# Rows of modulation panels moved, a first weight split moved to GpSimd, and a gate moved behind a rotation, in a two-block transformer kernel

## The chip, the cores and the metric

The kernel runs on one core of a Trainium2 chip. The metric is device time in microseconds (us) for one execution, lower is better. A core has TensorE (PE, matmuls; its weight loads are shown as PEld), VectorE (DVE), ScalarE (ACT), GpSimd (POOL), the SyncE queue (SP), and 16 DMA engines that the queues share.

## What is computed

Two diffusion-transformer blocks run one after the other on 256 latent tokens (with 256 context tokens), width 1024, all in float32. The first block has two layers. Each projects a modulated RMS norm of both streams, does two attentions (a low-rank one, MLA, and a neighbourhood one), merges them through gates, and ends with an MLP:

```python
mod_lat = (silu_c @ w_ada[l] + b_ada[l])[:, None, :]
sh1, sc1, gt1, sh2, sc2, gt2 = jnp.split(mod_lat, 6, axis=-1)
h = modulate(rms_norm(x_lat, g_attn[l]), sh1, sc1)
gl, mq, mk, mv, nq, nk, nv = mixer_proj(h, *proj_w)
...
g = jax.nn.sigmoid(gate_logits)
y = g[..., :D_MODEL] * (y_mla @ w_mla_o) + g[..., D_MODEL:] * (y_na @ w_na_o)
x_lat = x_lat + gt1 * (y @ w_out)
x_lat = x_lat + gt2 * squared_relu_mlp(modulate(rms_norm(x_lat, g_mlp[l]), sh2, sc2), w_ff1[l], w_ff2[l])
```

The second block has an mLSTM layer and then a windowed attention layer with 16 query heads and 4 key heads, rotary angles, a sink, and an output gate `silu(z)`, with its own modulation from `ada_w_2`.

## The kernel before

**Number format.** Every weight panel is split on chip into a high part (`whi`, written by ACT in `hi`, line 1106, as float32r) and the rest (`wlo`, a subtraction in `lo_to` on DVE, line 1664, or in `lo` on POOL, line 2285, for the panels named in `POOL_PANELS`). A product takes three matmuls: high by high, high by low, low by high (lines 552 to 554, 573 to 575, 589 to 591, 1024 to 1026). Activations are split the same way.

**Panels.** All weights come as panels of up to 1 MB (`plan`, line 135), in one fixed order, through three raw buffers. SP issues them in order (line 512). It may issue panel i only when panel i-3 has been given back: a weight panel is given back when its second low half is written, a modulation panel ("ada") when TensorE has multiplied with it, since it is used from the raw buffer as it is. `whi` and `wlo` have two buffers each, so the high part of weight n waits until TensorE has finished with weight n-2. In each half panel, TensorE can begin once the first half of the low part is there.

**Modulation.** There are 72 ada panels, numbered by `ADA`; four of them make one row of 1024 modulation values (shift, scale or gate). The first eight (`AT_START`) are at the front; the others are placed behind the weight panels listed in `AFTER`, and TensorE multiplies with each as soon as it is done with that weight (`used`, `ada`, line 606). ACT copies a finished row (`ada_out`, line 1118), TensorE turns it (`rows_out`, line 624) and DVE adds the bias (line 1671).

**The start.** ACT squares the eight chunks of both streams, DVE adds them up (`stat`), TensorE sums over partitions (`rms`, line 635), ACT takes the root, DVE the reciprocal (line 1706). Then `modulate` on DVE (line 1721) goes by chunks k = 0 to 7 of context ("c") and then latents ("l"): `scaled` for k and k+1, `left` for k. ACT writes the high part in `shifted` (line 1156). For odd k, POOL writes the low part in `norm_mod` (line 2295). `scaled` of chunk k waits for the low part of chunk k-4. TensorE takes the first projection panel `cq 0` chunk by chunk in `weight_pair` (lines 573 to 575), the next one, `cq 1`, whole.

**The gates of layer 0.** For each quarter h = 0 to 3 TensorE goes through the panels `gm`, `gn` (8 chunks, 1 MB each), `mo`, `no` (4 chunks, 512 KB each).

**The attention layer.** TensorE projects keys and queries, then z panel 0 (`gate(0)`, banks `atz` 0 and 1), turns the four key heads (`akT`, line 1049), projects z panels 1 and 2, and turns the queries. PSUM banks are given out in turn among six, and TensorE waits until the last holder of a bank has been read. DVE multiplies z by its sigmoid in `gate` (line 2203), which is what reads the `atz` banks, and rotates the query heads in `rotated` (line 2198).

Of the kernel before, what the change touches and what calls it, by code (L numbers as in the profile page):

```python
# [9 lines left out]
ALU = mybir.AluOpType  # L10
# [71 lines left out]
def zones():  # L82
# [9 lines left out]


AT_START = 8
AFTER = ([(kind, 0, h) for h in range(4) for kind in ("gm", "gn", "mo")]
         + [(f"ff{kind}", 0, 4 * g + a) for kind, g in MLP_ORDER for a in range(4)]
         + [("na", 1, a) for a in range(1, 5)] + [(kind, a) for kind in ("mq", "mk") for a in range(4)]
         + [(kind, a) for a in range(4) for kind in ("mo", "mz")])
# [10 lines left out]
    return k % 2 == 1 and (s, x) != ("s0", "c")  # L109


POOL_PANELS = [("uq", 0, 0), ("ff1", 0, 0), ("ckv", 1, 0), ("uq", 1, 0), ("ff1", 1, 0), ("mq", 0), ("atkv", 0)]


class Panel:
# [160 lines left out]
def program(nc, d, out):  # L276
    with ExitStack() as ctx:
# [14 lines left out]
        done = Done()  # L292
# [226 lines left out]
        def tensor(e):  # L519
# [559 lines left out]

            e.wait_ge(*done("ones"))  # L1080
            e.wait_ge(s_const, 16)
            for i in range(AT_START - 1):
                ada(i)
            for x in "cl":
                rms("n1.0", x)
            ada(AT_START - 1)
            first_layer(0)
            first_layer(1)
            lstm_layer()
# [3 lines left out]
        def scalar(e):  # L1093
# [144 lines left out]
            def first_layer(l):  # L1238
# [3 lines left out]
                tiles = [2, 3] if last else [0, 1, 2, 3]  # L1242
                s = f"n1.{l}"
                if not l:
                    for x in "cl":
                        for k in range(8):
                            shifted(s, k, x, "b", 0, 0)
                            if x == "c" and k == 1:
                                hi_to(at["cq", 0, 0].i)
                turned(s, "cl")  # L1250
                for x, kind in enumerate(("ckv", "cq") if last else ("cq", "ckv")):
                    h, gain, c0, acc, n_p = (cqh, S(f"gqa{l}"), q0, 2, 3) if kind == "cq" else (ckh, S(f"gkva{l}"), 0, 3, 1)
# [371 lines left out]
            e.wait_ge(s_x["lat"], 16)  # L1624
            for k in range(8):
                stat("n1.0", k, "cl")
                if k == 4:
                    ada_out(3)
            for x in "cl":
                rms("n1.0", x)  # L1630
            ada_out(AT_START - 1)
            first_layer(0)
            first_layer(1)
            lstm_layer()
# [3 lines left out]
        def vector(e):  # L1638
            nxt, rows, taken = [0], [0], [AT_START]

            def own():

                e.wait_ge(ve.sem, ve.n)
# [190 lines left out]
            def first_layer(l):  # L1834
# [5 lines left out]
                if not l:  # L1840
                    rows_out()
                    fold("b", 0, 1, "gattn0")
                    own()
                    modulate(s, "c", "b", 0, 1, 0, [(lambda: None, lambda: lo_to(at["cq", 0, 0].i))])
                    modulate(s, "l", "b", 0, 1, 0)
                ts(gcol[:, 0], S(f"gmqc{l}"), 96 ** -0.5, None, ALU.mult, None)
                e.tensor_copy(gcol[:, 1], S(f"gmkc{l}")).then_inc(*up(ve, ("gcol", l)))
                e.wait_ge(s_const, 16)
# [341 lines left out]
            def attention_layer():  # L2190
                s = "s1"
                tmp = work[:, :, :].rearrange("p a t -> p (a t)")
                ts(nsink[:, :], S("sink"), -1.0, None, ALU.mult, None)
                cs = C("rope2").rearrange("p (t s f) -> p t s f", t=2, s=2)
                for i, n in enumerate(("atq", "atk")):
                    rope_tables(atabs[:, i], cs, S(n)[:, 0:32], S(n)[:, 32:64])

                def rotated(v, n_h, i, tile, *names):
                    tm = [tmp[:, 512 * k:512 * k + n_h * 32].rearrange("p (h f) -> p h f", f=32) for k in range(4)]
                    tab = [atabs[:, i, k, tile].unsqueeze(1).to_broadcast([128, n_h, 32]) for k in range(4)]  # L2200
                    rope(v[:, :, 0:32], v[:, :, 32:64], tab, tm, *names)

                def gate(a):
                    for c in range(2 * a, 2 * a + 2):
                        e.wait_ge(*done(("asig", c)))
                        tt(sz[:, c, :], banks(("atz", c))[:, 0:256], sz[:, c, :], ALU.mult, ("read", ("atz", c)))

                begin(at["atkv", 0])
                begin(at["atkv", 1])
                for tile in range(4):  # L2210
                    e.wait_ge(*done(("aksq", tile)))
                    e.tensor_reduce(ass_[:, 0, tile], work[:, tile, 0:256].rearrange("p (h e) -> p h e", e=64), AX.X,
                                    ALU.add).then_inc(*up(ve))
                rsqrt_fine(ass_[:, 1], ass_[:, 0], ass_[:, 2], 64, "aks", "akrt")
                for tile in range(4):
                    tt(qk[:, tile], qk[:, tile], ass_[:, 1, tile].unsqueeze(2).to_broadcast([128, 4, 64]), ALU.mult)
                begin(at["atq", 0])
                own()
                for tile in range(4):
                    v = qk[:, tile]  # L2220
                    if tile < 2:
                        tt(v, v, S("atk").unsqueeze(1).to_broadcast([128, 4, 64]), ALU.mult)
                    else:
                        rotated(v, 4, 1, tile - 2)
                    own()
                    e.tensor_copy(kd[:, tile, :, 0, :], v).then_inc(*up(ve))
                    e.tensor_copy(kd[:, tile, :, 1, :], v).then_inc(*up(ve, ("k heads", tile)))
                begin(at["atq", 1])
                for half in range(2):
                    r = slice(half * 8, half * 8 + 8)  # L2230
                    for tile in range(2):
                        e.wait_ge(*done(("aqsq", half, tile)))
                        e.tensor_reduce(asums[:, tile, r], aPT[half][:, tile, :].rearrange("p (h e) -> p h e", e=64), AX.X,
                                        ALU.add).then_inc(*up(ve))
                    rsqrt_fine(arms[:, :, r], asums[:, :, r], ascr[:, :, r], 64, ("aqs", half), ("aqrt", half))
                    begin(at["atz", 0] if half else at["atq", 2])
                    if half:
                        gate(0)
                    for tile in range(2):
                        rotated(aqtok[:, tile, half * 512:half * 512 + 512].rearrange("p (h e) -> p h e", e=64), 8, 0, tile,  # L2240
                                ("q heads", half))
                        if tile == 0 and half == 0:
                            begin(at["atq", 3])
                for a in range(1, 3):
                    begin(at["atz", a])
                    gate(a)
                own()

                def among_units(i):
                    if i == 1:  # L2250
                        gate(3)
                    if i in (16, 17):
                        lo_to(at["atw", i - 16].i)

                softmax("A", at_units(), ast, among_units)
                gate_lo(7)
                for a in range(4):
                    begin(at["atw", a])
                    for j in range(2):
                        residual("at", 2 * a + j, ("atw", 2 * a + j), "s", 1, 2, "l")  # L2260
# [20 lines left out]
        def gpsimd(e):  # L2281
            def lo(p):
                for a in range(2):
                    e.wait_ge(*done(("hi", p.i, a)))
                    e.tensor_tensor(p.half(wlo[p.buf], a), p.half(raw[p.slot], a), p.half(whi[p.buf], a).bitcast(F32),  # L2285
                                    ALU.subtract).then_inc(*up(po, ("lo", p.i, a)))

            def rsqrt(o, i, ready, *names):

                e.wait_ge(*done(ready))  # L2290
                e.tensor_scalar(o, i, EPS, None, ALU.add).then_inc(*up(po))
                e.wait_ge(po.sem, po.n)
                e.tensor_tensor(o, o, power[:, :], ALU.pow).then_inc(*up(po, *names))

            def norm_mod(s, parts):
                for x in parts:
                    a, b, _ = PARTS[x]
                    for k in range(1, 8, 2):
                        e.wait_ge(*done(("xhi", s, k, x)))
                        e.tensor_tensor(XAl[:, k, a:b], work[:, k % 4, a:b], XAh[:, k, a:b].bitcast(F32), ALU.subtract).then_inc(  # L2300
                            *up(po, ("xlo", s, k, x)))

            for l in range(2):
                q0 = CTX if l else 0
                if l:
                    lo(at["ckv", l, 0])
                norm_mod(f"n1.{l}", "cl")
                lo(at["uq", l, 0])
                lo(at["ff1", l, 0])
                norm_mod(f"n2.{l}", "l" if l else "cl")  # L2310
            lo(at["mq", 0])
            e.wait_ge(*done(("ff2 end", 1, 3)))
            e.wait_ge(*done(("sum", "s0", "l")))
            e.dma_start(zone[:, :], d["zones"]).then_inc(s_zone, 16)
            norm_mod("s0", "l")
            for i in range(16):
                ssc = col[:, i % 4, 14:15]
                rsqrt(ssc, ssc, ("h mean", i), ("h root", i))
            lo(at["atkv", 0])
            norm_mod("s1", "cl")  # L2320
# [71 lines left out]
```

## Time and profile before

| | |
|---|---|
| median of 3 runs | 2172.58 us (2172.06 to 2174.23) |
| the profiled execution, its own time | 2172.58 us |
| its span in the profile | 2170.8 us |
| PE busy | 2077.5 us, 96% |
| DVE busy | 1132.4 us, 52% |
| ACT busy | 906.0 us, 42% |
| POOL busy | 79.3 us, 4% |
| mean granted TensorE clock | 0.984 |
| read from HBM | 273.01 MB, 127 GB/s |

The span is the time between the first and the last instruction; the device time has 1.8 us more around it. Busy times of different engines overlap. A bracket behind a row of a timeline is the idle time of that engine before it, and what ended it. A granted clock of 1.00 is 2.4 GHz, 0.50 is 1.2 GHz.

### The profile page before, as it was taken

Reading aid. Unit: us, or ns where it says so; the run is one execution under the profiler, and the core shown is the slowest. Engines: PE = TensorE matmul, PEld = TensorE weight load, DVE = VectorE, ACT = ScalarE, POOL = GpSimd, SP = SyncE. Lnnn points to the kernel's source line nnn. Section 1 sums busy time; section 2 is a strip of 40 time slices with the busy share of each in tenths; the row PEclk is TensorE's granted clock in tenths of the full one; section 3 lists DMA queues with packets and bytes.
Section 4 is the critical chain, followed back from the end, with each engine's and each line's share of the span. In section 5 each row is a group of like instructions: output and inputs, shape, how many; then the busy total and the mean of one; then the engine's idle time right before and its main releaser. Section 6 shows DMA issues by size and latency. Waiting matters only on the chain.

```text
span 2170.8 us, 32405 instructions
## 1 busy us (share of the span) xinstructions
PE 2077.5 (96%) x13362; PEld 1727.6 (80%) x13362; DVE 1132.4 (52%) x2150; ACT 906.0 (42%) x1639; POOL 79.3 (4%) x91
## 2 busy tenths in 40 slices
PE   5998999999999999999999899999999799999998
PEld 3897767778777777798779899987877577888977
DVE  4447562336433343465555677642466444445876
ACT  4445662324322231255564555433333222233575
POOL 1000000002000000110000100010000000001000
PEclk8999999999999999999999999999999999999999
DMA  7222004642444444344105445444211044222311
GB/s 282 102 88 75 34 18 148 220 158 78 165 184 155 187 163 168 143 165 180 54 35 197 173 182 186 176 157 160 117 59 57 2 174 175 90 105 78 117 59 40
DMA packets 47106, 277.19 MB, mean 128 GB/s; under 512 B 4464, under 2 KB 12784, under 8 KB 16752
## 3 DMA queue, kind: packets, MB, share of 16 engines
q1 hardware_dynamic: 42080, 266.94, 32.6%
q10 hardware_dynamic: 4736, 7.34, 1.0%
q8 instruction: 106, 1.74, 0.3%
q0 software_dynamic: 144, 0.85, 0.1%
q14 instruction: 40, 0.33, 0.0%
HBM read 273.01 MB, written 2.10 MB: 127 GB/s over the span
## 4 chain that ended last, share of the span: by engine, by line
PE 85%; DVE 7%; ACT 4%; DMA 1%; issue 1%; POOL 0%; SPq 0%; ACTq 0%; DVEq 0%
PE ps L552 18%; PE ps L553 18%; PE ps L554 18%; PE ps L589 4%; PE ps L590 4%; PE ps L591 4%; PE ps L669 3%; PE ps L619 3%; PE ps L705 2%; PE ps L692 2%; DVE t L1646 2%; PE ps L983 2%; DVE t L1664 2%; DMA t<-in_panels 1%; DVE t L1655 1%
## 5 line engine op out<-in xcount | busy, mean ns | idle before, releaser
L552 PE MATMUL ps<-t 128*128 128x512 f32 (+1 forms) x2232 | 779.7, 349 | 6.4 <-DVE t L1664 4.2
L553 PE MATMUL ps<-t 128*128 128x512 f32 (+1 forms) x2232 | 770.4, 345 | 0.0
L554 PE MATMUL ps<-t 128*128 128x512 f32 (+1 forms) x2232 | 769.9, 345 | 0.0
L1664 DVE TENSOR_TENSOR t<-t 128x1024 fp32r<-128x1024 f32 (+2 forms) x364 | 407.4, 1162 | 440.6 <-ACT t L1106 439.9
L1106 ACT ACTIVATE t<-t 128x1024 fp32r<-128x1024 f32 (+2 forms) x378 | 359.6, 1000 | 368.9 <-DMA t<-in_panels 293.1
L552 PEld LDWEIGHTS ps<-t 128*128 128x128 f32 x2232 | 422.3, 189 | 84.0 <-issue 17.1
L554 PEld LDWEIGHTS ps<-t 128*128 128x128 f32 x2232 | 422.3, 189 | 52.9
L553 PEld LDWEIGHTS ps<-t 128*128 128x128 f32 x2232 | 422.5, 189 | 50.1
L1646 DVE TENSOR_TENSOR t<-t 128x512 f32<-128x512 f32 (+9 forms) x637 | 249.3, 411 | 196.2 <-ACT t L1195 51.8
L589 PE MATMUL ps<-t 128*128 128x256 f32 (+1 forms) x812 | 241.2, 297 | 0.3 <-DVE t L1664 0.3
L590 PE MATMUL ps<-t 128*128 128x256 f32 (+1 forms) x812 | 234.8, 289 | 0.0
L591 PE MATMUL ps<-t 128*128 128x256 f32 (+1 forms) x812 | 234.7, 289 | 0.0
L1195 ACT ACTIVATE t<-ps 128x256 f32<-128x256 f32 (+1 forms) x254 | 113.2, 458 | 284.5 <-PE ps L554 154.7
L589 PEld LDWEIGHTS ps<-t 128*128 128x128 f32 x812 | 157.1, 193 | 8.1 <-issue 3.3
L590 PEld LDWEIGHTS ps<-t 128*128 128x128 f32 x812 | 157.0, 193 | 3.2 <-issue 1.7
L591 PEld LDWEIGHTS ps<-t 128*128 128x128 f32 x812 | 157.0, 193 | 1.4
L1655 DVE SCALAR_TENSOR_TENSOR t<-ps,t 128x256 f32<-128x256 f32 (+2 forms) x176 | 83.1, 496 | 112.1 <-PE ps L554 92.7
L1646 DVE TENSOR_TENSOR t<-ps,t 128x512 f32<-128x512 f32 (+5 forms) x150 | 63.1, 427 | 113.0 <-ACT t L1229 56.5
L619 PE MATMUL ps<-t 128*32 128x256 f32 x1152 | 82.1, 405 | 16.9 <-DMA t<-in_panels 16.2
L1218 ACT ACTIVATE t<-ps,t 128x512 f32<-128x512 f32 (+1 forms) x128 | 86.8, 688 | 13.4 <-DVE t L1646 11.5
L1655 DVE SCALAR_TENSOR_TENSOR t<-t 128x256 f32<-128x256 f32 (+5 forms) x194 | 82.5, 456 | 12.6 <-ACT t L1164 10.4
L2285 POOL TENSOR_TENSOR t<-t 128x1024 fp32r<-128x1024 f32 (+1 forms) x14 | 31.8, 2295 | 1556.7 <-ACT t L1106 1556.7
(149 smaller groups left out, 1793.4 us busy)
## 6 DMA issues: line engine op xcount, KB each, us to landing
t<-in_panels SPq DMA_DIRECT2D x236, 1024.0 KB, 4.8
t<-in_panels SPq DMA_DIRECT2D x19, 512.0 KB, 4.3
t<-in_panels SPq DMA_DIRECT2D x6, 768.0 KB, 4.3
t<-in_window ACTq DMA_DIRECT2D x4, 768.0 KB, 4.2
t<-in_ctxT SPq DMA_DIRECT2D x1, 1024.0 KB, 12.4
t<-in_xT SPq DMA_DIRECT2D x1, 1024.0 KB, 14.7
t<-in_ctxT ACTq DMA_DIRECT2D x1, 1024.0 KB, 5.6
t<-in_xT ACTq DMA_DIRECT2D x1, 1024.0 KB, 7.3
```

The source lines that it names most:

```text
L552: e.matmul(o, hi[:, k, w], xh[:, c0:c1], start=k == 0, stop=False)
L553: e.matmul(o, hi[:, k, w], xl[:, c0:c1], start=False, stop=False)
L554: t = e.matmul(o, lo[:, k, w], xh[:, c0:c1], start=False, stop=k == p.nk - 1)
L589: e.matmul(o, xh[:, r], hi[:, k, n0:n1], start=k == 0, stop=False)
L590: e.matmul(o, xh[:, r], lo[:, k, n0:n1], start=False, stop=False)
L591: t = e.matmul(o, xl[:, r], hi[:, k, n0:n1], start=False, stop=k == p.nk - 1)
L619: t = e.matmul(o[32 * j:32 * j + 32, 0:256], sc[kind][:, 2 * q + k, :], w[:, k, j * 256:j * 256 + 256], start=q == 0 and k == 0, stop=q == ...
L1106: e.activation(p.half(whi[p.buf], a), p.half(raw[p.slot], a), ACT.Copy).then_inc(*up(se, ("hi", p.i, a)))
L1195: e.activation(o, i, func, scale=scale).then_inc(*up(se, ("read", key), *names))
L1646: e.tensor_tensor(o, a, b, op).then_inc(*up(ve, *names))
L1655: e.scalar_tensor_tensor(o, a, s_, b, o1, o2).then_inc(*up(ve, *names))
L1664: e.tensor_tensor(p.half(wlo[p.buf], a), p.half(raw[p.slot], a), p.half(whi[p.buf], a).bitcast(F32), ALU.subtract).then_inc(*up(ve, ("lo", ...
```

## The change

Five edits, in four places of the program.

1. `AFTER`: in layer 0 the twelve ada panels 8 to 19 stood behind `gm`, `gn`, `mo` of h = 0 to 3; now they stand behind `gm`, `gn`, `mo`, `no` of h = 0 to 2. The order of the load, of TensorE's work, of `ada_out` and of `rows_out` follows.
2. The low part of the first weight panel, `cq 0` of layer 0, is made on POOL in place of DVE, ahead of POOL's first `norm_mod`.
3. At the start TensorE multiplies with ada panels 0 to 3, does both `rms` sums, and then ada panels 4 to 7; before, ada 0 to 6, the sums, ada 7. ACT copies row 0 behind the last square, ahead of the roots, in place of amid the squares.
4. ACT writes the high part of `cq 0` ahead of all `shifted` chunks, in place of behind chunk 1.
5. In the attention layer DVE's `gate(0)` moves from ahead of the rotation of the second half of the query heads to behind it.

```diff
-AFTER = ([(kind, 0, h) for h in range(4) for kind in ("gm", "gn", "mo")]
+AFTER = ([(kind, 0, h) for h in range(3) for kind in ("gm", "gn", "mo", "no")]
...
-POOL_PANELS = [("uq", 0, 0), ...
+POOL_PANELS = [("cq", 0, 0), ("uq", 0, 0), ...
@@ tensor
-            for i in range(AT_START - 1):
+            for i in range(4):
                 ada(i)
             for x in "cl":
                 rms("n1.0", x)
-            ada(AT_START - 1)
+            for i in range(4, AT_START):
+                ada(i)
@@ scalar, first_layer
                 if not l:
+                    hi_to(at["cq", 0, 0].i)
                     for x in "cl":
                         for k in range(8):
                             shifted(s, k, x, "b", 0, 0)
-                            if x == "c" and k == 1:
-                                hi_to(at["cq", 0, 0].i)
@@ scalar, start
             for k in range(8):
                 stat("n1.0", k, "cl")
-                if k == 4:
-                    ada_out(3)
+            for i in range(4):
+                ada_out(i)
             for x in "cl":
                 rms("n1.0", x)
-            ada_out(AT_START - 1)
+            for i in range(4, AT_START):
+                ada_out(i)
@@ vector, first_layer
+                    lo_to(at["cq", 0, 0].i)
                     own()
-                    modulate(s, "c", "b", 0, 1, 0, [(lambda: None, lambda: lo_to(at["cq", 0, 0].i))])
-                    modulate(s, "l", "b", 0, 1, 0)
+                    for x in "cl":
+                        modulate(s, x, "b", 0, 1, 0)
@@ vector, attention_layer
                     begin(at["atz", 0] if half else at["atq", 2])
-                    if half:
-                        gate(0)
                     for tile in range(2):
                         rotated(aqtok[...], 8, 0, tile, ("q heads", half))
...
-                for a in range(1, 3):
-                    begin(at["atz", a])
+                for a in range(3):
+                    if a:
+                        begin(at["atz", a])
                     gate(a)
@@ gpsimd
-                if l:
-                    lo(at["ckv", l, 0])
+                lo(at["ckv" if l else "cq", l, 0])
                 norm_mod(f"n1.{l}", "cl")
```

## Rows read from the trace of the kernel before

**Rows 1.** The page: busy time of TensorE; and its chain, by engine.
```profile
PE 2077.5 (96%) x13362; PEld 1727.6 (80%) x13362; DVE 1132.4 (52%) x2150; ACT 906.0 (42%) x1639; POOL 79.3 (4%) x91
...
PE 85%; DVE 7%; ACT 4%; DMA 1%; issue 1%; POOL 0%; SPq 0%; ACTq 0%; DVEq 0%
```

**Rows 2.** Timeline, all engines, 2061.5 to 2064.6: start, duration, engine, line, tiles, count.
```profile
2061.83 1.91 PE L1049 MATMUL ps<-t 128*128 128x128 f32 x16
...
2063.28 0.75 DVE L1646 TENSOR_TENSOR t<-ps,t 128x256 f32<-128x256 f32 x2
...
2063.81 0.19 PEld L552 LDWEIGHTS ps<-t 128*128 128x128 f32 x1 [0.30 <-DVE t L1646]
```

**Rows 3.** Timeline of DVE from 2060 to 2105.
```profile
2061.00 2.36 DVE L1664 TENSOR_TENSOR t<-t 128x1024 fp32r<-128x1024 f32 x2
...
2064.06 4.49 DVE L1646 TENSOR_TENSOR t<-t 128x256 f32<-128x256 f32 x12
```

**Rows 4.** Timeline of TensorE: first matmul after two idle times.
```profile
55.80 0.50 PE L552 MATMUL ps<-t 128*128 128x512 f32 x1 [1.53 <-DVE t L1664]
...
914.45 1.19 PE L640 MATMUL ps<-t 128*128 128x256 f32 x2 [4.50 <-DVE t L1646]
```

**Rows 5.** Windows: busy time of each engine, granted clock, DMA share, GB/s.
```profile
24.00:26.00 2.00, 2.00 (x17) 0.60 (x17) 1.70 (x3) 1.57 (x3) 0.00 (x0) 0.50 1.02 410
...
914.00:915.00 1.00, 0.55 (x1) 0.50 (x2) 0.30 (x1) 0.00 (x0) 0.02 (x1) 0.50 0.00 0
...
918.00:919.00 1.00, 1.00 (x7) 1.00 (x7) 0.90 (x3) 0.42 (x2) 0.00 (x0) 0.64 0.00 0
```

**Rows 6.** Timelines of TensorE and ScalarE, layer 0, from 381 to 388.
```profile
381.15 0.51 PE L552 MATMUL ps<-t 128*128 128x512 f32 x1
...
385.80 0.55 ACTq L1399 DMA_DIRECT2D t<-in_xT  x1
...
386.94 1.07 PE L619 MATMUL ps<-t 128*32 128x256 f32 x16
...
387.94 0.50 PE L552 MATMUL ps<-t 128*128 128x512 f32 x1
```

**Rows 7.** Timelines in the MLP of layer 0, four engines, from 556 to 566.
```profile
556.54 1.07 PE L619 MATMUL ps<-t 128*32 128x256 f32 x16
...
557.67 0.80 SPq L512 DMA_DIRECT2D t<-in_panels  x2
...
562.34 2.01 ACT L1106 ACTIVATE t<-t 128x1024 fp32r<-128x1024 f32 x2 [3.65 <-DMA t<-in_panels]
...
563.44 2.36 DVE L1664 TENSOR_TENSOR t<-t 128x1024 fp32r<-128x1024 f32 x2 [4.02 <-ACT t L1106]
```

**Rows 8.** Timelines at the start of the kernel, three engines, in order of time.
```profile
23.04 0.38 ACT L1125 ACTIVATE t<-ps 128x256 f32<-128x256 f32 x1 [0.94 <-PE ps L619]
...
24.03 2.34 DVE L1646 TENSOR_TENSOR t<-t 128x512 f32<-128x512 f32 x3 [1.00 <-ACT t L1143]
...
24.10 3.86 PE L619 MATMUL ps<-t 128*32 128x256 f32 x32
...
31.08 3.54 DVE L1706 RECIPROCAL t<-t 128x256 f32<-128x256 f32 x2 [4.71 <-ACT t L1153]
...
31.73 1.07 PE L619 MATMUL ps<-t 128*32 128x256 f32 x16
...
34.95 1.09 DVE L1655 SCALAR_TENSOR_TENSOR t<-t 128x16 f32<-128x16 f32 x3
...
36.95 1.99 ACT L1106 ACTIVATE t<-t 128x1024 fp32r<-128x1024 f32 x2
...
41.35 1.28 DVE L1655 SCALAR_TENSOR_TENSOR t<-t 128x256 fp32r<-128x256 f32 x3 [0.18 <-ACT t L1164]
```

**Rows 9.** Timelines of POOL and DVE ahead of the attention layer.
```profile
1991.71 4.93 POOL L2285 TENSOR_TENSOR t<-t 128x1024 fp32r<-128x1024 f32 x2 [267.19 <-ACT t L1106]
...
1993.16 1.23 DVE L1646 TENSOR_TENSOR t<-t 128x256 f32<-128x256 f32 x1 [0.54 <-ACT t L1143]
```

More of the change, by code:

```diff
@@ L109, in on_pool @@
     return k % 2 == 1 and (s, x) != ("s0", "c")
-POOL_PANELS = [("uq", 0, 0), ("ff1", 0, 0), ("ckv", 1, 0), ("uq", 1, 0), ("ff1", 1, 0), ("mq", 0), ("atkv", 0)]
+POOL_PANELS = [("cq", 0, 0), ("uq", 0, 0), ("ff1", 0, 0), ("ckv", 1, 0), ("uq", 1, 0), ("ff1", 1, 0), ("mq", 0), ("atkv", 0)]
 class Panel:
@@ L2201, in rotated @@
                     rope(v[:, :, 0:32], v[:, :, 32:64], tab, tm, *names)
[L2203 to L2206, printed above, removed]
                 begin(at["atkv", 0])
@@ L2243, in attention_layer, with gate @@
                             begin(at["atq", 3])
-                for a in range(1, 3):
-                    begin(at["atz", a])
+                def gate(a):
+                    for c in range(2 * a, 2 * a + 2):
+                        e.wait_ge(*done(("asig", c)))
+                        tt(sz[:, c, :], banks(("atz", c))[:, 0:256], sz[:, c, :], ALU.mult, ("read", ("atz", c)))
+                for a in range(3):
+                    if a:
+                        begin(at["atz", a])
                     gate(a)
```

## The prediction

> **What bounds the kernel now.** I read the page first, for who is busy. TensorE is, 96% of the span, and the chain that ended last runs 85% through it [rows 1]. So an edit on another engine counts only where it makes TensorE wait, and there it counts in full, for there is next to nothing later in which a wait could be absorbed. I then took the four places of the change one by one, with the timeline of each engine, and asked for each TensorE instruction what it needs and when that is there. The three that matter are the attention layer, the gates of layer 0, and the start. The profiled execution took 2172.58 us, which is also the median, around a span of 2170.8 us, so differences of the span carry over one to one.
>
> **Edit 5, the gate behind the rotation.** The reader should look at TensorE between 2061 and 2064. It turns the four key heads from 2061.83 for 1.91 us, to 2063.74 [rows 2]. Then comes z panel 1. PSUM banks are dealt in turn among six: `atz` 0 and 1, then four `akT`, so `atz` 2 falls on the bank of `atz` 0, and must wait until DVE has read it. DVE reads it in `gate(0)`, two multiplications from 2063.28 to 2064.03, the first done at about 2063.7. TensorE's weight load starts at 2063.81, and it names DVE as what it waited for, 0.30 us [rows 2]. So this wait ends last already, by a hair: there is no slack at all. After the edit DVE ends the split at 2063.36, then does the rotation, twelve operations in 4.49 us [rows 3], and only then `gate(0)`. The first read ends at 2063.3 + 4.5 + 0.4 = 2068.2 in place of 2063.7, and z panel 1 begins 4.5 us late. What gets earlier is the rotated query heads, by 0.75 us. TensorE turns those only behind z panels 1 and 2, some 12 us later, so that is worth nothing. DVE's next split (for z panel 2) comes 0.1 us later, ahead of z panel 1's end by 5 us. Cost: 4.5 us.
>
> The idle time has a second price. Before 914.45 TensorE had idled 4.50 us, about as long [rows 4]; behind it the granted clock was 0.50 and came back within the slice from 918 to 919, whose mean is 0.64, so at 918.7 [rows 5]. For 4.3 us it did half of what it could, which costs 1.7 to 2.1 us. Idle times of a third of that are common in this trace (1.53 us before 55.80 [rows 4]) with the clock at full speed behind them, so I charge this loss to the long stall alone. I take 1.9 us here. If the clock is not lowered, this term is nothing; if it is, 2.1 at most. Edit 5 together: 6.4 us, between 4.4 and 6.6.
>
> **Edit 1, the ada panels of layer 0.** Twelve stay twelve, each still 1.0 us of TensorE (386.94 to 387.94 [rows 6]), so TensorE's work is the same. What moves is who waits for which buffer. Panel i is loaded when panel i-3 is given back. Before, `gm` of quarter h+1 follows `mo`, ada, `no`, and so waits for `mo`'s low part, long done. After, the order is `mo`, ada, `no`, ada, `gm`: it waits for the ada panel behind `mo`, that is until TensorE is done with it. From there to a `gm` that can be multiplied, the MLP has the same pattern: the ada panel ends at 556.54 + 1.07 = 557.61, SP issues at 557.67, the panel has landed when ACT starts on it at 562.34, DVE starts on the low part at 563.44 and has half of its 2.36 us done at 564.62 [rows 7]. That is 7.0 us. In the MLP 11 us of matmuls cover it. Here the cover is `no`: a panel of that size takes 386.94 - 381.15 = 5.8 us, and the ada panel another 1.0 [rows 6], in which the first 0.07 overlap. 6.7 us of cover for 7.0 us: 0.3 to 0.4 us of stall, for h = 0, 1, 2. For h = 1 ACT issues the 1 MB load of `xT` in this stretch, right behind the split of `no` (at 385.80 [rows 6]). It shares the engines with `gm`'s load. At the 410 GB/s of a full stretch [rows 5] one MB takes 2.6 us; a third of that, 0.9 us, is my estimate of the overlap, between nothing and 2.6. Quarter 3 now has no ada panels, but its loads were covered before, so nothing comes back. Rows of modulation are complete earlier, and none was waited for. Sum: 3 x 0.35 + 0.9 = 1.9 us, between 0.5 and 4.
>
> **Edits 2, 3 and 4, the start.** Before, TensorE's two norm sums stood behind ada 6, which waited for its load, and the reciprocals began at 31.08 [rows 8]. DVE's last addition ends at 26.37. With row 0's copy no longer amid the squares (0.94 us idle and 0.38 us of copy on ACT, 1.00 us idle on DVE [rows 8]) it ends at about 25.4. The reciprocals can begin at about 27.0 (I allow 1.6 us for sum and root, an estimate) and end at 30.6 in place of 34.6. That is a gain of 4 us only if the modulation row is there, and here lies the catch. Ada 7 is loaded when ada 4 has been used. Ada 4 started at 24.10, now it stands behind both sums and row 0's turn, at about 28.3. At the granted clock of 0.50 one such panel takes 1.93 us (two took 3.86 [rows 8, 5]), so it is given back at 30.2 in place of 26.0, the load lands 4.7 us later [rows 7], and ada 7 starts at 34.9 in place of 31.73 [rows 8]. Copy, turn and bias take to 37.3, so the first `scaled`, which followed the three operations begun at 34.95 at about 35.2, starts at 37.5.
>
> `cq 0` comes late as well: its slot is that of ada 5, given back at 31.9, and it cannot land before 36.6, more likely at 37.4 since ada 7 lies ahead in the queue. ACT now waits for it ahead of every `shifted`; its split took 1.99 us from 36.95 [rows 8]. Its first half is done at 38.4. DVE is rid of 2.36 us, but POOL takes 4.93 us for the same two halves [rows 9], to 43.4, and its part of `norm_mod` comes behind it: chunk 1's low part at 44.0 or 44.2 (0.6 us by the same rate). `scaled` of chunk 5 waits for it. Before, that was the last of the three operations from 41.35, starting at 42.2 [rows 8]. From there the chunks go at their old pace, so `modulate`, POOL's last chunk, ACT's split of `cq 1` and TensorE's start on it, at 55.80 before [rows 4], all come 1.9 us late. Without POOL's queue it would still be 37.5 against 35.2 less the DVE work saved, about nothing. I take 2.0 us, between -1 and 4.
>
> POOL's work could also slow DVE down. While POOL made such a low part, a DVE addition of two 128x256 tiles took 1.23 us [rows 9], against 4.49 / 12 = 0.37 us in the rotation [rows 3]. Five chunk operations fall under `cq 0`'s split; at 0.86 us more each they would take 4.3 us more, of which 1.9 us are idle on DVE already, waiting for chunk 1: 2.4 us more. This is how the Trainium skill has it (GPSIMD Engine Reference, Key points): the two engines share their interfaces to SBUF, and contend when a DVE instruction has two inputs there. By that rule the start would cost 4.4 us and not 2.0. I keep the 2.0, because these operations also wait for ACT between one another.
>
> **Sum.** 6.4 + 1.9 + 2.0 = 10.3 us: 2172.6 + 10.3 = 2182.9 us.
>
> **Rivals.**
> - *No clock loss, small stalls* (edit 5 at 4.5, edit 1 at 1, start at 0): 2178 us. For it: only one idle time of this length is in my rows. Chance 0.16.
> - *Contention* (start by the DVE operations' stretched time, `gm` behind `xT` in full): 2.4 + 2 more, 2187 us. The 1.23 us speaks for it. Chance 0.13.
> - *The start pays and edit 5 is all that stands against it*: if ada 7 lands by 32, the earlier reciprocals and DVE's 2.36 us give back up to 4 us, and with 4.5 for edit 5 the time is 2173 to 2176, no change. It needs ada 4 to be given back by 27.5, ahead of the sums. Chance 0.05.
> - *The other side, faster*: as the last, and z panel 1 does not wait, because its bank is not the one that `gate(0)` frees. Then 2172.6 - 4 = 2168.6 us. It decides with one fact, the bank, and the 0.30 us wait for DVE speaks against it. Chance 0.02.
> - *The forecast*, 2180 to 2186 us: 0.64.
>
> **How the numbers follow.** The range takes the forecast and most of the two rivals beside it: 2177.5 to 2187.5. A measurement of this kernel can tell about 0.2%, 4.3 us, from no change, so "slower" begins at 2176.9 us. Faster 0.02, same 0.05, slower 0.93.
>
> **What would show it.** Edit 5: TensorE idle for 4.4 us or so at the first matmul of z panel 1, released by DVE's multiplication, followed by some 4 us at a granted clock of 0.50. Edit 1: three waits of TensorE for the low part of `gm`, h = 1 to 3, 0.3 us each, the second the longest, where before there was none. Start: ada 7 near 35, POOL's split of about 5 us from 38.5, the first matmul of `cq 1` near 57.8. I am wrong if z panel 1 starts without a wait, if ada 7 starts before 33, or if `gm`'s loads land in under 4.5 us.

## The result, and the profile of the changed kernel

The changed kernel took 2189.88 us (median of 4, 2188.52 to 2192.39), the kernel before beside it 2172.32 us (4 runs, 2168.26 to 2174.23): ratio 1.0085, 95% interval 1.0068 to 1.0101. That is 17.6 us slower, where 10.3 were predicted, and above the top of the range, 2187.5. The same kernel measured a second time gave the same ratio (below). The profiled execution took 2195.78 us, 5.9 us above the median, around a span of 2193.9 us. So I read a second profile of the kernel too (span 2189.9 us).

The page of the changed kernel, TensorE's row and the chain, against [rows 1]:

```profile
PE 2082.4 (95%) x13362; PEld 1730.7 (79%) x13362; DVE 1133.4 (52%) x2148; ACT 905.7 (41%) x1639; POOL 84.2 (4%) x93
...
PE 83%; DVE 8%; ACT 5%; DMA 2%; issue 1%; POOL 0%; SPq 0%; ACTq 0%; DVEq 0%
```

The span grew by 23.1 us. TensorE is busy for 4.9 us of those with the same instructions (a lower clock); the rest is idle time. Where it lies is seen in TensorE's timeline, at the first matmuls behind idle times (the bracket is the idle time and what ended it), of the changed kernel:

```profile
21.18 1.93 PE L619 MATMUL ps<-t 128*32 128x256 f32 x16 [6.74 <-DMA t<-in_panels]
...
25.67 1.22 PE L640 MATMUL ps<-t 128*128 128x256 f32 x2 [2.56 <-DVE t L1647]
...
36.45 1.07 PE L619 MATMUL ps<-t 128*32 128x256 f32 x16 [3.60 <-DMA t<-in_panels]
...
42.97 0.55 PE L573 MATMUL ps<-t 128*128 128x256 f32 x1 [4.26 <-DVE t L1656]
...
45.95 0.58 PE L573 MATMUL ps<-t 128*128 128x256 f32 x1 [1.37 <-POOL t L2302]
...
60.54 0.50 PE L552 MATMUL ps<-t 128*128 128x512 f32 x1 [1.05 <-DVE t L1665]
...
366.41 0.79 PE L552 MATMUL ps<-t 128*128 128x512 f32 x1 [2.75 <-DVE t L1665]
...
410.75 0.79 PE L552 MATMUL ps<-t 128*128 128x512 f32 x1 [3.43 <-DVE t L1665]
...
452.21 0.50 PE L552 MATMUL ps<-t 128*128 128x512 f32 x1 [0.51 <-DVE t L1665]
...
2085.69 0.36 PE L552 MATMUL ps<-t 128*128 128x256 f32 x1 [4.62 <-DVE t L1647]
```

Lines from 1080 on have moved by one or two: 1647, 1656 and 1665 of DVE were 1646, 1655 and 1664. The first six rows are the start: ada 3, the norm sums, ada 7, chunk 0, chunk 1, `cq 1`. The next three are `gm` of h = 1, 2 and 3, none of which waited before. The last is z panel 1.

The same points in both profiles of the changed kernel, as what each stretch adds to the lag behind the profile of before:

| stretch | predicted | first profile | second profile |
|---|---|---|---|
| start, up to `cq 1` | 2.0 | 4.7 | 6.4 |
| from there to the gates of layer 0 | 0 | 0.9 | 0.0 |
| gates and the MLP's norm, 332 to 517 before | 1.9 | 12.6 | 6.2 |
| from there to z panel 1 | 0 | -1.0 | 0.6 |
| attention: stall, over that of before | 4.5 | 4.5 | 4.5 |
| attention: behind the stall | 1.9 | 1.3 | 1.3 |
| sum (of the spans) | 10.3 | 23.1 | 19.1 |

The rows are rounded, the sums are those of the spans. Edit 5 was right but for 0.6 us of clock. The other two terms were too small, and the one of the gates differs by 6 us from one execution to the next. What makes the stretch between the MLP's norm and z panel 1 differ by 1.6 us is not known.

**The attention layer**, DVE's timeline, TensorE's first weight load of z panel 1, and the windows of the changed kernel (columns as in [rows 5]):

```profile
2080.72 4.49 DVE L1647 TENSOR_TENSOR t<-t 128x256 f32<-128x256 f32 x12
2085.12 0.75 DVE L1647 TENSOR_TENSOR t<-ps,t 128x256 f32<-128x256 f32 x2
...
2085.66 0.19 PEld L552 LDWEIGHTS ps<-t 128*128 128x128 f32 x1 [4.83 <-DVE t L1647]
```

```profile
2083.00:2085.60 2.60, 0.00 (x0) 0.00 (x0) 2.57 (x8) 0.74 (x1) 0.00 (x0) 1.00 0.68 287
...
2085.70:2087.00 1.30, 1.30 (x7) 1.30 (x8) 1.30 (x3) 0.00 (x0) 0.00 (x0) 0.61 0.04 13
2087.00:2088.00 1.00, 1.00 (x7) 1.00 (x6) 1.00 (x2) 0.00 (x0) 0.00 (x0) 0.50 0.00 0
```

The rotation stands ahead of `gate(0)`, its 4.49 us are those of [rows 3], and TensorE starts when the gate's first multiplication is done. The 0.30 us of [rows 2] was the wait of the weight load, so it is to be compared with 4.83 here: 4.5 us more (the 4.62 above is the idle time of the matmuls, which was 0.1 us before). The granted clock was still 1.00 during the wait and fell to 0.50 just behind it.

**The gates.** ScalarE and SP in the changed kernel: SP's issues for `gm` of h = 1 and 2 (with those behind them), ACT's split of `gm` for h = 1, 2, 3, and the load of `xT` (the 7.13 us of an SP row is the time over which its three issues are spread, no landing time):

```profile
356.92 7.13 SPq L512 DMA_DIRECT2D t<-in_panels  x3
...
364.04 2.00 ACT L1107 ACTIVATE t<-t 128x1024 fp32r<-128x1024 f32 x2 [8.59 <-DMA t<-in_panels]
...
398.13 0.55 ACTq L1399 DMA_DIRECT2D t<-in_xT  x1
...
400.59 7.13 SPq L512 DMA_DIRECT2D t<-in_panels  x3
...
408.39 2.00 ACT L1107 ACTIVATE t<-t 128x1024 fp32r<-128x1024 f32 x2 [9.11 <-DMA t<-in_panels]
...
449.84 2.01 ACT L1107 ACTIVATE t<-t 128x1024 fp32r<-128x1024 f32 x2 [6.04 <-DMA t<-in_panels]
```

The chain is the one predicted: ada panel, SP, load, ACT, DVE, TensorE. The load is not: issued at 356.92 it lands at 364.04, 7.1 us, and issued at 400.59, 2.5 us behind `xT`'s, it lands at 408.39, 7.8 us. Only the third took 4.9 us (SP's issue at 444.96), against the 4.7 that I took for all. The packets that began in the first 3.4 us behind `gm`'s issue, by queue (packets, MB, share of the engines' time; q1 is SP's queue, with the panels, q10 is ScalarE's, with `xT`), for h = 2 (400.6 to 404) and then for h = 3 (445 to 448.4):

```profile
q10 hardware_dynamic: 746, 0.75, 74.9%
q1 hardware_dynamic: 10, 0.08, 27.2%
...
q1 hardware_dynamic: 101, 0.81, 67.0%
```

So the two loads did not share: `xT`, issued 2.5 us earlier, had 0.75 MB begin in this time and `gm` 0.08 MB, where `gm` of h = 3 had 0.81 MB. `xT` goes in small packets (1040 for 1.05 MB). Windows of the changed kernel show the second price:

```profile
370.00:372.00 2.00, 2.00 (x6) 1.61 (x5) 1.50 (x3) 0.44 (x1) 0.00 (x0) 0.50 0.71 287
...
373.00:374.00 1.00, 1.00 (x6) 0.84 (x5) 0.55 (x1) 1.00 (x2) 0.00 (x0) 1.00 0.06 25
...
415.00:416.00 1.00, 1.00 (x3) 0.75 (x3) 0.84 (x2) 0.09 (x1) 0.00 (x0) 0.50 0.90 320
```

Behind both long stalls the clock is at its lower level, 0.50, for about 6 us, and `gm` takes 14.2 us, twice, in place of the 11.4 that it takes for h = 1 in the second profile, with the clock full. Stalls of 2.75 + 3.43 + 0.51 us and 2 x 2.8 us make 12.3 of the 12.6.

**The start.** ScalarE's split of `cq 0`, then GpSimd and DVE in the changed kernel; the last row is the view that groups instructions by line and shape from 41.4 to 45.4 (its second operation is cut off by the window), with busy time and mean ns:

```profile
39.05 2.00 ACT L1107 ACTIVATE t<-t 128x1024 fp32r<-128x1024 f32 x2 [1.09 <-DMA t<-in_panels]
...
40.19 4.85 POOL L2287 TENSOR_TENSOR t<-t 128x1024 fp32r<-128x1024 f32 x2 [39.76 <-ACT t L1107]
...
41.49 1.33 DVE L1656 SCALAR_TENSOR_TENSOR t<-t 128x256 fp32r<-128x256 f32 x1 [1.44 <-ACT t L1165]
...
42.74 2.58 DVE L1656 SCALAR_TENSOR_TENSOR t<-t 128x256 f32<-128x256 f32 x1
...
46.90 0.47 DVE L1656 SCALAR_TENSOR_TENSOR t<-t 128x256 f32<-128x256 f32 x1
```

```profile
L1656 DVE SCALAR_TENSOR_TENSOR t<-t 128x256 f32<-128x256 f32 x2 | 3.4, 1758 | 0.0
```

In the kernel before such an operation takes 0.48 us (1.28 for three, [rows 8]). Here one takes 1.33 and the next 2.58 us. GpSimd's two instructions of 2.43 us (the mean) end at 42.5 and 45.0, and DVE's two end at 42.8 and 45.3, each 0.3 us behind one of them. A third takes 0.94 us beside chunk 1's low part. That is not a stretch by a factor: DVE waited until the GpSimd instruction was over, the first time for the rest of one, the second time for nearly a whole one. The Trainium skill states this outright (SBUF — State Buffer, SBUF: two separate sides): of the two engines, the one that starts first has the shared ports for the whole instruction and the other is blocked, for DVE operations with two SBUF inputs. The trace agrees, with these two rows.

The row at 46.90 is `scaled` of chunk 5. It may start when chunk 1's low part is there, which was at 45.90, so it was not this wait that ended last but DVE's own blocked operations, by 1.0 us. In the second profile the first two `scaled` were blocked, 4.99 us for the two, and GpSimd was free again before chunk 1 was ready for it.

### The profile page after: what moved, and what is told of

It reads as the page before. It is cut to its first block, busy times and chain, and to the rows that moved or that the text cites. A ratio compares the mean times of both kernels' runs of the same rounds, so it can differ in the third digit from the quotient of the medians.

```text
span 2193.9 us, 32405 instructions
## 1 busy us (share of the span) xinstructions
PE 2082.4 (95%) x13362; PEld 1730.7 (79%) x13362; DVE 1133.4 (52%) x2148; ACT 905.7 (41%) x1639; POOL 84.2 (4%) x93
## 4 chain that ended last, share of the span: by engine, by line
PE 83%; DVE 8%; ACT 5%; DMA 2%; issue 1%; POOL 0%; SPq 0%; ACTq 0%; DVEq 0%
PE ps L552 18%; PE ps L553 17%; PE ps L554 17%; PE ps L589 4%; PE ps L590 4%; PE ps L591 4%; PE ps L669 3%; PE ps L619 3%; DVE t L1647 2%; PE ps L705 2%; PE ps L692 2%; PE ps L983 2%; DVE t L1665 2%; DVE t L1656 2%; DMA t<-in_panels 2%
## 5 line engine op out<-in xcount | busy, mean ns | idle before, releaser
L2287 POOL TENSOR_TENSOR t<-t 128x1024 fp32r<-128x1024 f32 (+1 forms) x16 | 36.7, 2316 | 1609.3 <-ACT t L1107 1609.3
```

## The experiments

Theories ahead of the runs: *A*, each edit costs what its own buffer or queue makes it wait for, and the costs add up; with it that `xT`'s load delays `gm`, and that ada 7 is late because ada 4 is given back late. *B*, the costs come from something else (the number of ada panels close together, the sums ahead of panels, edits that act only together). The count of executions stands beside each time.

**One edit at a time, on the kernel before (2174.58 us, 26 runs, beside these four).** Edit 5 alone (`gate(0)` behind the rotation):

> Edit 5 alone on the kernel before. Theory: z panel 1 waits 4.5 us for its bank and then about 4 us pass at a granted clock of 0.50, together 6 us, so 2178 us. Rival (the stall is absorbed in the attention that follows, or the clock loss is hidden): 2172 to 2176 us.

2180.44 us (9 runs), ratio 1.0025 [1.0015, 1.0035], 5.9 us more. TensorE's timeline:

```profile
2070.76 0.36 PE L552 MATMUL ps<-t 128*128 128x256 f32 x1 [4.62 <-DVE t L1646]
```

The same stall as in the whole change, and 5.8 us more lag behind the layer than ahead of the stall: 4.5 of stall and 1.3 of clock. The clock fell behind the stall, at about 2071, and was full again at about 2074.6.

Edit 1 alone:

```diff
-AFTER = ([(kind, 0, h) for h in range(4) for kind in ("gm", "gn", "mo")]
+AFTER = ([(kind, 0, h) for h in range(3) for kind in ("gm", "gn", "mo", "no")]
```

> Edit 1 alone. Theory from the trace after: the panel gm of quarters 1, 2 and 3 arrives late by 2.8, 3.4 and 0.5 us, and after each of the two long stalls the granted clock costs another 2.7 us; 12 us in all, 2184 us. Rival A (my prediction): 0.35 us a stall and 0.9 us for the load of xT, 2174 to 2175 us. Rival B: the late landing for quarter 1 (7.1 us from issue) was a chance event of the one profiled execution; then about 6.5 us, 2179 us, and the landing is 4.7 us here.

2180.31 us (6 runs), ratio 1.0030 [1.0017, 1.0042], 5.7 us more, where 1.9 had been predicted, and 12 expected from the stalls of the first profile. Nearest is rival B, 6.5 us: `gm` for h = 1 took 5.7 us to land here, not 7.1, and its stall was 1.28 us, not 2.75. The same with the load of `xT` in the last quarter of layer 0 in place of the second:

```diff
-                    if h == 1:
+                    if h == (1 if last else 3):
                         src = kept
```

> Edit 1 alone, and the load of xT that ACT issues in quarter 1 of layer 0 is issued in quarter 3. Theory that this load makes gm of quarter 2 late: its stall falls from 3.4 us to that of an undisturbed quarter (0.5 us), and its clock loss goes, so 5 to 6 us less than edit 1 alone. Rival (the gm panels are late whatever runs beside them, as in quarter 1): within 1 us of edit 1 alone, the stall stays near 3 us.

2175.72 us (10 runs), ratio 1.0005 [0.9995, 1.0014], 1.1 us more. The timelines of TensorE at `gm` of h = 1, 2, 3, first with `xT` in its place, then with it moved:

```profile
359.35 0.50 PE L552 MATMUL ps<-t 128*128 128x512 f32 x1 [1.28 <-DVE t L1664]
...
401.78 0.79 PE L552 MATMUL ps<-t 128*128 128x512 f32 x1 [4.34 <-DVE t L1664]
...
442.56 0.50 PE L552 MATMUL ps<-t 128*128 128x512 f32 x1 [0.37 <-DVE t L1664]
```

```profile
364.17 0.50 PE L552 MATMUL ps<-t 128*128 128x512 f32 x1 [1.21 <-DVE t L1664]
...
402.66 0.50 PE L552 MATMUL ps<-t 128*128 128x512 f32 x1 [0.41 <-DVE t L1664]
...
441.24 0.50 PE L552 MATMUL ps<-t 128*128 128x512 f32 x1 [0.49 <-DVE t L1664]
```

Of the stalls only the second differs: 4.34 us with `xT`'s load beside `gm`'s, 0.41 without. From the end of the ada panel to ACT's split it was 8.8 us with and 4.8 without. The stall takes the lower clock with it (0.79 us for the first matmul in place of 0.50). So `xT`'s load costs 4.6 of edit 1's 5.7 us by the medians, a little less than expected; between the two profiles the gates differ by 6.2 us. What is left is 1.1 us by the medians, with an interval from -1 to 3. That this is the prediction's 3 x 0.35 is luck: the profile has 1.21 + 0.41 + 0.49 = 2.1 us of stalls, most of it for h = 1.

Edits 2, 3 and 4 together (the start):

> Edits 2, 3 and 4 together, without 1 and 5. Theory from the trace after: the first matmul of cq 1 is 4.7 us later than before, so 2177 us. Rival (my prediction): 2.0 us, 2174 to 2175 us. If the three parts are independent, the sum of the differences of this run and of the two others is that of the whole change, 17 to 18 us.

2178.12 us (10 runs), ratio 1.0017 [1.0008, 1.0027], 3.5 us more. The three parts add up to 15.1 us of 17.6, which the intervals (about 2 us each way on every part) allow.

**The whole change again, its start taken apart, and the whole with `xT` moved (before: 2173.01 us, 19 runs).**

> The changed kernel as it is, a second time, to see which of its stalls repeat. Theory: the late landings of gm in quarters 1 and 2 are in part chance, as the 7.1 us of quarter 1 were 5.7 us with edit 1 alone; here quarter 1 lands 4.8 to 7 us after its issue, quarter 2 nearly 8 or 9 us, quarter 3 near 4.9 us. Time 2188 to 2193 us. Rival: the start makes the queue later, and 7.1 us in quarter 1 comes back to within 0.3 us.

2192.46 us (4 runs), ratio 1.0085 [1.0068, 1.0102]: confirmed. Its profile is the second one of the table. TensorE there, at ada 7, chunk 0, `gm` for h = 1 and 2, and z panel 1:

```profile
38.04 1.94 PE L619 MATMUL ps<-t 128*32 128x256 f32 x16 [5.30 <-DMA t<-in_panels]
...
47.14 0.55 PE L573 MATMUL ps<-t 128*128 128x256 f32 x1 [5.99 <-DVE t L1656]
...
365.16 0.50 PE L552 MATMUL ps<-t 128*128 128x512 f32 x1 [0.77 <-DVE t L1665]
...
406.82 0.80 PE L552 MATMUL ps<-t 128*128 128x512 f32 x1 [3.55 <-DVE t L1665]
...
2081.61 0.36 PE L552 MATMUL ps<-t 128*128 128x256 f32 x1 [4.61 <-DVE t L1647]
```

The stalls beside `xT` (3.55) and in the attention layer (4.61) repeat. The one for h = 1 does not: 0.77 us with the clock full behind it, against 2.75 and 2.8 us of slow matmuls. Its load is the slow one in all five profiles that have edit 1: 5.1 to 7.1 us from SP's issue, against 4.7 to 4.9 us for h = 2 and 3 without `xT` beside them. What makes it slow, and vary, stays open.

> The changed kernel with the load of xT of layer 0 issued in quarter 3 in place of quarter 1. With edit 1 alone this took 4.6 us off. Theory: the same here, 4 to 7 us below the changed kernel, 2184 to 2186 us, the stall of quarter 2 near 0.4 us and its clock loss gone. Rival: with two other edits in the kernel the stall is cause of less, under 2 us.

2185.62 us (4 runs), ratio 1.0061 [1.0044, 1.0078], 6.8 us below the whole change beside it. The stall for h = 2 is 0.41 us there. So `xT`'s load is a piece of the size of edit 5's 5.9 us; which of the two is larger the intervals don't tell.

Edit 3 alone, and edits 2 and 4 alone:

> Edit 3 alone: ada 0 to 3, both sums, ada 4 to 7. Theory: ada 7 starts 4 to 5 us late, since its load waits for ada 4 which now stands behind the sums, and that is most of what the start costs: 2 to 4 us, 2177 to 2178 us. Rival (what costs is the split on GpSimd and its queue): under 1 us here.

> Edits 2 and 4 without 3: the first weight's low part on GpSimd, its high part ahead of the modulated chunks. Theory: the chunks wait for GpSimd's 4.9 us, but DVE is rid of 2.4 us, so it costs 0 to 2 us. Rival (this is what the start costs): 3 us and more.

Edit 3: 2178.17 us (10 runs), ratio 1.0022 [1.0012, 1.0031], 5.2 us more (2 to 4 expected). Edits 2 and 4: 2174.37 us (10 runs), ratio 1.0004 [0.9995, 1.0014]. So it is the order of the panels that costs. (That edit 3 alone shows more than 2, 3 and 4 together, 5.2 against 3.5 us, is within the intervals.) Edits 2 and 4 cost 1.4 us at most likely, and no change can't be excluded. In their profile `cq 1` comes 37.6 us behind ada 3, 2.8 more than before, but ada 7 is 2.2 us later there already, with the panels in their old order: a slow load, not the edits.

**What in edit 3, and what would repair it (before: 2174.15 us, 33 runs).** One ada panel more ahead of the sums:

```diff
-            for i in range(4):
+            for i in range(5):
                 ada(i)
             for x in "cl":
                 rms("n1.0", x)
-            for i in range(4, AT_START):
+            for i in range(5, AT_START):
                 ada(i)
```

> Edit 3 alone, but with ada 0 to 4 ahead of the norm sums and ada 5 to 7 behind them, in place of 0 to 3 and 4 to 7. Theory (the start is late because ada 4 is given back late, and ada 7 is loaded into its buffer): ada 4 is given back some 5 us after ada 3 begins, as before, ada 7 starts within 11.5 us of ada 3 (before 10.7, with edit 3 as made 14.8), the first matmul of cq 1 comes 34.5 to 36 us after ada 3 (before 34.75), and the time is that of the kernel before, 0 to 1.5 us above it. Rival (it is the sums ahead of panels, or row 0's copy behind the squares, that costs): 4 to 5 us above, as with edit 3 alone.

2175.57 us (11 runs), ratio 1.0003 [0.9994, 1.0012], 1.4 us more: the loss is gone, within the interval. TensorE's ada 3, ada 7 and `cq 1`, first with edit 3 as made, then with five panels ahead:

```profile
22.09 1.93 PE L619 MATMUL ps<-t 128*32 128x256 f32 x16 [7.33 <-DMA t<-in_panels]
...
36.84 1.93 PE L619 MATMUL ps<-t 128*32 128x256 f32 x16 [2.56 <-DMA t<-in_panels]
...
61.05 0.50 PE L552 MATMUL ps<-t 128*128 128x512 f32 x1 [1.53 <-DVE t L1666]
```

```profile
22.73 1.94 PE L619 MATMUL ps<-t 128*32 128x256 f32 x16 [7.34 <-DMA t<-in_panels]
...
34.13 1.07 PE L619 MATMUL ps<-t 128*32 128x256 f32 x16 [0.73 <-DMA t<-in_panels]
...
57.24 0.50 PE L552 MATMUL ps<-t 128*128 128x512 f32 x1 [1.54 <-DVE t L1666]
```

Counted from ada 3, ada 7 starts 14.8 us later in the first and 11.4 in the second (10.7 before), and `cq 1` 39.0 and 34.5 (34.75 before). The sums stand ahead of panels and row 0's copy behind the squares in both, so neither is the cause. The buffer of ada 4 is. The earlier sums buy nothing: the modulation row comes no sooner.

Edit 1 with the ada panels behind `gm`, `gn`, `no` of all four quarters, never behind `mo`:

> The twelve ada panels of layer 0 behind gm, gn and no of h = 0 to 3, so never behind mo; on the kernel before. Theory (edit 1 costs because gm's buffer is that of the ada panel behind mo): gm of the next quarter waits only for mo's low part, so no stall of TensorE over 0.3 us at gm, xT's load meets no load that is waited for, no change: within 1 us of the kernel before. Rival (any ada panel close ahead of gm costs, because the loads of gm and the ada panels share the DMA engines): stalls of 1 to 4 us at gm as in edit 1, 2 to 6 us slower.

2174.01 us (11 runs), ratio 1.0000 [0.9991, 1.0009], and no idle time of TensorE over 0.3 us from 334 on in the gates, with `xT` where it was. An ada panel stands right ahead of `gm` here too (though three to a quarter and not four), and `gm` waits for `mo`'s buffer: it is the buffer that counts. `gm`'s load is then issued early, and `xT` finds nothing that is waited for.

Edit 2 alone, ScalarE's order as before:

> Edit 2 alone: the low part of cq 0 on GpSimd ahead of norm_mod, ScalarE's split of cq 0 where it was, behind chunk 1. Theory (GpSimd's 4.9 us ahead of chunk 1's low part hold the chunks up, whatever ScalarE's order): cq 1 comes 2 to 3.5 us later after ada 3 than before, the time is 1 to 3 us above. Rival (it is ScalarE's wait for cq 0 ahead of the shifted chunks that costs in edits 2 and 4): no change, within 0.7 us.

2175.94 us (11 runs), ratio 1.0009 [1.0000, 1.0019], 1.8 us more. GpSimd and DVE there, then TensorE at chunk 1 and `cq 1`:

```profile
39.84 4.84 POOL L2286 TENSOR_TENSOR t<-t 128x1024 fp32r<-128x1024 f32 x2 [39.41 <-ACT t L1106]
...
41.14 3.82 DVE L1655 SCALAR_TENSOR_TENSOR t<-t 128x256 fp32r<-128x256 f32 x2 [1.81 <-ACT t L1164]
```

```profile
45.60 0.58 PE L573 MATMUL ps<-t 128*128 128x256 f32 x1 [1.71 <-POOL t L2301]
...
58.76 0.50 PE L552 MATMUL ps<-t 128*128 128x512 f32 x1 [0.78 <-DVE t L1664]
```

From ada 3 (22.54) `cq 1` comes 36.2 us later, 1.5 more than before, less than the 2 to 3.5 expected. Two DVE operations again take 3.82 us in place of 1.0, and here DVE then waits another 0.62 us for chunk 1's low part. The lean is that it is GpSimd's split and not ScalarE's order, though the interval begins at no change.

All three repairs on the changed kernel (ada behind `gm`, `gn`, `no`; five panels ahead of the sums; `gate(0)` back), with edits 2 and 4 kept:

> The changed kernel with three repairs: ada panels of layer 0 behind gm, gn, no; five ada panels ahead of the sums; gate(0) back ahead of the rotation. Edits 2 and 4 stay. Theory: what is left is the price of edits 2 and 4, 1 to 2 us above the kernel before (2174 to 2175), 14 to 17 us below the changed kernel. Rival (the edits cost something together that no part shows, the sum of the parts having been 15.1 of 17.6 us): 3 to 5 us above the kernel before. If the sums early and the low part on GpSimd help one another, it is below the kernel before.

2175.43 us (11 runs), ratio 1.0005 [0.9996, 1.0014]: 1.3 us above the kernel before, 14 to 17 us below the changed one. The rival, 3 to 5 us left over, is not seen. Whether edits 1, 3 and 5 as made cost something together this run can't tell, since the repairs take all three away; against it speaks that the table of stretches finds nearly all of the loss at the places of the edits. No version tried is faster than the kernel before.

## Why the prediction was wrong, by its own steps

- **Edit 5, right.** 4.5 us of stall predicted, 4.5 found (4.83 for 0.30 at the weight load). The clock: 1.9 predicted, 1.3 found in all three profiles. The edit alone measured 5.9 us for 6.4.
- **Edit 1, the mechanism right, two sizes wrong.** The waits are those for `gm` behind the ada panel, the second the longest. The term that failed is "a third of that, 0.9 us, is my estimate of the overlap", with its bound of 2.6 us: `xT`'s load put 3 to 4 us on `gm`'s, not 0.9 (7.8 us against 4.9 in the first profile, a stall of 4.34 against 0.41 in the edit alone). The estimate had the two loads share the engines; in the trace `gm` had 0.08 MB begin in 3.4 us and `xT` 0.75 MB. The bound of 2.6 us divided bytes by the 410 GB/s of a full stretch [rows 5], while the engines moved 246 GB/s in the mean in those 3.4 us. Second, "landed 4.7 us later" came from a single row [rows 7]; it was right for h = 3, and for h = 1 it was 5.1 to 7.1 us. With 0.3 us of margin missing, each of those goes to the stall in full.
- **The clock, charged in one place and due in three.** "I charge this loss to the long stall alone" failed. My rows had 1.53 us with the clock full and 4.50 with it halved, and nothing between. In the gates, stalls of 2.75, 3.43, 3.55 and 4.34 us all had the low clock behind them, and 1.28 did not. That is 5.6 us of the first profile. An unknown between two rows should have stood in the range, tied to the size of the stalls.
- **The start, the path right, too short.** Ada 7 was to start at 34.9 and started at 36.45: ada 4 stood behind both sums and began at 29.0, not 28.3, and its successor took 5.4 us to come (SP's issue at 31.03), not 4.7; in the second profile it took 7.0 (31.08 to 38.04). `cq 0` behind it landed at 39.05, not at 37.4, and ScalarE had waited 1.09 us for it. So POOL's split, put at 38.5, started at 40.19, and chunk 1's low part, put at 44.0 or 44.2, was there at 45.9: 1.7 us of the 2.7 missed (`cq 1` came at 60.54, not 57.8). The step that failed is, for the most part, again the landing time of 4.7 us. The other 1.0 us is the next item.
- **Contention of GpSimd and DVE, a rival that I sized wrongly.** I took 0.86 us more for each of five operations, and then left it out of the sum. It was three operations of 1.33, 2.58 and 0.94 us, each blocked to the end of a GpSimd instruction, 3.4 us more in all. That "these operations also wait for ACT between one another" did not hide it: `scaled` of chunk 5 began 1.0 us behind the low part that it was said to wait for. So the block cost 1.0 us beyond the queue on GpSimd in the first profile. The rule of the Trainium skill named ahead (GPSIMD Engine Reference, Key points) named the right cause, but that its 4.4 us lie close to the 4.7 found is luck: most of what was missing came from landing times.
- **Nothing found for the other side.** No gain was measured on any edit.

## What to carry to other kernels

Moving a small panel between loads moves the moment at which a buffer comes free, and it is that moment that costs. Before such a move, write down for each late load which item gave its buffer back, and move panels only to where that item is long done; both repairs here (behind `no`, never `mo`; a fifth panel ahead of the sums) changed one such owner and brought the time back to within 1.5 us. When the cover of a load is within 1 us of its landing time, take the spread of landing times from many rows and look for any other queue's load in the window, and count with the clock's loss (1.3 to 2.8 us here) behind every stall of the size of those here, 2.75 us and more.

## What the runs showed of the hardware that was not expected

- Landing times of 1 MB loads of the same shape: 4.7 to 7.1 us from the issue, and 7.8, 7.9 and 8.7 us beside `xT`'s load, issued 2.2 to 2.5 us earlier on another queue. In the 3.4 us behind `gm`'s issue 0.75 MB of `xT` began, in packets of 1 KB, and 0.08 MB of `gm`; without `xT` it was 0.81 MB. Its bytes at 410 GB/s explain 2.6 us, and it cost 3 to 4.
- In the gates and the attention layer TensorE's granted clock was 0.50 behind stalls from 2.75 us up, for 3 to 6 us afterwards, and 1.00 behind stalls of up to 1.28 us. About the same stall cost 2.8 us of slow matmuls in one execution (3.43 us) and 1.3 in another (3.55 us), where the clock was back some 3 us sooner. The length of the stall alone does not decide: at the start of the first profile ada 7, behind 3.60 us of idle time, ran at the full clock (1.07 us), which fell 1.5 us later.
- A DVE operation with two SBUF inputs that takes 0.48 us alone took up to 2.58 us beside GpSimd subtractions of 2.43 us in the mean, and ended 0.3 us behind them.
